# A two-layer encoder with product-key retrieval: eight more tokens take their down products from gathered rows, and half of a search moves ahead

## The reference, cut to what is computed

```python
def peer(h, w_q, sub_keys, w_down, w_up):
    q = (ht @ w_q).reshape(T, PEER_HEADS, 2, PEER_HALF_DIM)           # 8 heads, 2 halves of 128
    scores = jnp.einsum('thic,hikc->thik', q, sub_keys)               # 128 keys per half
    sv, si = lax.top_k(scores, PEER_TOPK)                             # 16
    cand = sv[:, :, 0, :, None] + sv[:, :, 1, None, :]
    best, ci = lax.top_k(cand.reshape(T, PEER_HEADS, 256), PEER_TOPK)
    ...
    expert = i1 * PEER_N_KEYS + i2                                    # 16384 experts, 128 of them per token
    gate = softmax(best)
    hid = gelu(einsum('cd,ckd->ck', x, w_down[expert]))
    return einsum('ck,ckd->cd', gate * hid, w_up[expert])
```

## Time and profile before

| | |
|---|---|
| time, median of 3 runs | 1514.79 us (1514.16 to 1517.17) |
| the profiled execution, its own time | 1503.53 us |
| its span, first to last instruction | 1501.7 us |
| TensorE busy | 1479.2 us, 98% |
| VectorE busy | 892.0 us, 59% |
| GpSimd busy | 716.5 us, 48% |
| DMA, whole span | 523.12 MB, mean 348 GB/s |
| mean granted TensorE clock | 0.997 |

### The profile page before, as it was taken

How to read it: one execution, slowest core, us unless ns; L and a number is a source line. 1 busy time by engine, 2 the same in 40 slices (tenths; PEclk the granted TensorE clock), 3 DMA queues, 4 the chain that set the end, 5 groups by cost and what they waited for, 6 DMA issues and landing times.

```text
span 1501.7 us, 29008 instructions
## 1 busy us (share of the span) xinstructions
PE 1479.2 (98%) x10648; PEld 1440.7 (96%) x10648; DVE 892.0 (59%) x2921; ACT 473.2 (32%) x1184; POOL 716.5 (48%) x632
## 2 busy tenths in 40 slices
PE   8999999999999999999999999999999999999996
PEld 6889999999999999999978999999999999999996
DVE  1740999948885444444623449997588834444363
ACT  6663231248881000000055533121788500000001
POOL 6577033448994333333467831333699723332350
PEclk9999999999999999999999999999999999999998
DMA  7356999999999999999845679999999999999993
GB/s 257 133 204 235 332 339 364 409 408 342 383 389 407 416 416 417 416 417 415 360 150 200 211 244 351 349 407 408 367 375 385 383 416 415 416 417 416 417 404 141
DMA packets 126416, 523.12 MB, mean 348 GB/s; under 512 B 14816, under 2 KB 15072, under 8 KB 109536
## 3 DMA queue, kind: packets, MB, share of 16 engines
q1 hardware_dynamic: 56896, 240.27, 42.0%
q0 software_dynamic: 55296, 201.35, 34.3%
q10 hardware_dynamic: 14112, 80.04, 13.1%
HBM read 519.48 MB, written 1.05 MB: 347 GB/s over the span
## 4 chain that ended last, share of the span: by engine, by line
PE 94%; POOL 1%; DMA 1%; issue 1%; ACT 1%; DVE 1%; DVEq 0%; POOLq 0%; SPq 0%; ACTq 0%
PE ps L992 93%; POOL w_lo L605 1%; DMA spare<-in_wu 1%; PE ps L1000 1%; ACT hT_hi L707 0%; DMA raw<-in_wm 0%; DMA xs<-in_x 0%; ACT w_hi L692 0%; ACT arena L680 0%; DVE arena L1385 0%; DVE rtmp L1374 0%; DVE arena L1523 0%; POOL arena L630 0%; PE ps L1322 0%; PE ps L1120 0%
## 5 line engine op out<-in xcount | busy, mean ns | idle before, releaser
L992 PE MATMUL ps<-arena,raw 128*128 128x160 f32 (+1 forms) x2688 | 377.4, 299 | 0.2
L992 PE MATMUL ps<-arena,w_raw 128*128 128x160 f32 (+1 forms) x2688 | 377.3, 299 | 0.0
L992 PEld LDWEIGHTS ps<-arena,raw 128*128 128x128 f32 x2688 | 368.1, 190 | 0.7 <-issue 0.7
L992 PEld LDWEIGHTS ps<-arena,w_raw 128*128 128x128 f32 x2688 | 368.2, 190 | 0.0
L622 POOL DMA_INDIRECT arena<-in_up_rows,ret x192 | 188.1, 979 | 355.1 <-DVE oh_buf L1697 263.3
L622 POOL DMA_INDIRECT arena<-in_rows,ret x192 | 200.0, 1042 | 285.8 <-ACT ret L879 104.5
L1697 DVE SCALAR_TENSOR_TENSOR oh_buf<-arena,ret,oh_buf 128x1024 f32<-128x1024 f32 x126 | 161.8, 1284 | 227.9 <-DMA arena<-in_up_rows,ret 227.9
L605 POOL TENSOR_TENSOR w_lo<-raw,w_hi 128x1024 fp32r<-128x1024 f32 x80 | 194.0, 2436 | 90.8 <-PE ps L992 66.1
L992 PE MATMUL ps<-arena 128*128 128x160 f32 (+5 forms) x1336 | 184.5, 302 | 0.4 <-DMA spare<-in_wu 0.3
L992 PEld LDWEIGHTS ps<-arena 128*128 128x128 f32 (+2 forms) x1336 | 177.9, 189 | 4.0 <-issue 2.6
L1580 DVE SCALAR_TENSOR_TENSOR arena<-arena,ps 128x1024 f32<-128x1024 f32 x128 | 153.6, 1213 | 0.0
(11 more groups left out here) (149 smaller groups left out, 1780.6 us busy)
## 6 DMA issues: line engine op xcount, KB each, us to landing
raw<-in_wd SPq DMA_DIRECT2D x92, 512.0 KB, 6.8
w_raw<-in_wd SPq DMA_DIRECT2D x92, 512.0 KB, 7.6
raw<-in_wm SPq DMA_DIRECT2D x80, 512.0 KB, 3.4
low_rows<-in_wu SPq DMA_DIRECT2D x18, 1024.0 KB, 7.9
arena<-in_wu SPq DMA_DIRECT2D x18, 1024.0 KB, 7.9
arena<-in_wd SPq DMA_DIRECT2D x32, 512.0 KB, 4.9
raw<-in_wu SPq DMA_DIRECT2D x14, 1024.0 KB, 8.0
raw<-in_wu ACTq DMA_DIRECT2D x14, 1024.0 KB, 8.0
```

Of the source, the lines that this page charges most:

```text
L992: return nc.tensor.matmul(out, lhsT, rhs, start=start, stop=stop, skip_group_check=shared)
```

## The change

There are four parts.

Tokens 96 to 103 (`MID` = 8) leave the down products and not the up products. Their hidden values come from 8 more gathered rows a layer, each of which serves the 8 tokens in 16 groups of partitions; the rows of the tokens are copied to these groups by 16 more transfers of SP, and their ids spread by one more matmul before the block at which the 32 tokens' ids are spread. The down products have 152 columns (`DOWN_COLS`). VectorE spreads the hidden values (`spread_mid`), TensorE brings them to one column per token beside down block 97 (`with_mid`), VectorE multiplies them onto the gates (`gate_mid`), and the last two of the 40 gate groups, which are now those of the eight tokens, are written in place of multiplied.

The search of the first tile is split into heads 0 to 3 and heads 4 to 7. The scores of the first four heads are made before query block 10, and VectorE searches them while the query blocks run. Banks are changed for it (`SCORE_BANKS`, `search_psum`). Gathers can begin after the first half: pieces of indices at ScalarE's blocks 4, 7, 20 and 25. 44 rows are dotted early, in 20 places, six of them in the second half of the first tile's search. TensorE's product of the 64 tokens' rows, before block 8, now waits for the first half.

The early spread of ids moves from block 28 to 26, the turning of gates and ids from 77 to 76, the gate groups from 80 to 79. The 60 later rows are dotted over 47 blocks, where 56 were over 44.

VectorE copies and splits ids of tokens from 96 on only, and ScalarE writes its ones from block 34 on, not 16.

```diff
-RING, IN_FLIGHT = 10, 5
+RING, IN_FLIGHT, RING_FIRST = 10, 5, 2
+MID, MID_TO = 8, DENSE_FROM + 8
+DOWN_ROWS = ROWS + MID
+GATHERS = DOWN_ROWS + ROWS
+DOWN_COLS = DENSE - MID
-IDS_AT = 77
-TAKE_AT = 26
-PIECES, PIECE_AT = 4, (18, 21, 24, 26)
-MORE_AT, MORE_TAKE_AT, MORE_GATES_AT = 28, 33, 40
+IDS_AT = 76
+TAKE_AT = 28
+PIECES, PIECE_AT = 4, (4, 7, 20, 25)
+EARLY_SCORES_BEFORE, EARLY_HEADS = 10, RH // 2
+SCORE_BANKS = (0, 1, 0, 1, 4, 5, 6, 7)
+MORE_AT, MORE_TAKE_AT, MORE_GATES_AT = 26, 34, 40
-G_FROM = 80
+G_FROM = 79
-ONES_FROM, ROWS_AT, ONES = 12, 8, 432
-SPARSE_FIRST, MORE_LAST = 18, 10
-EARLY, EARLY_PLACES = SPARSE_FIRST + MORE - MORE_LAST, 14
+ONES_FROM, ROWS_AT, ONES = 30, 8, 432
+SPARSE_FIRST, MORE_LAST = 26, 14
+EARLY, EARLY_PLACES = SPARSE_FIRST + MORE - MORE_LAST, 20
+DOT_BLOCKS = BLOCKS - G_FROM - 2
 def dots_after(b):
-    return EARLY + max(0, min(ROWS - EARLY, (b - G_FROM - 1) * (ROWS - EARLY) // 44))
+    return EARLY + max(0, min(DOWN_ROWS - EARLY, (b - G_FROM - 1) * (DOWN_ROWS - EARLY) // DOT_BLOCKS))
...
+                for i in range(MID_PARTS):
+                    sp.dma_start(mid_rows[i * MID:(i + 1) * MID, :],
+                                 gff[DENSE_FROM:MID_TO, :]).then_inc(mid_rows_sb, 16)
...
+                    if q == RING - 1:
+                        pool.wait_ge(first_searched, l + 1)
...
                 take_queries(0)
-                high_parts(l * LAYER + Q_FROM + 12, l * LAYER + MIX_BLOCKS)
+                act.wait_ge(rinv_done, query_norm)
+                for b in range(Q_FROM + 12, MIX_BLOCKS):
+                    high(b)
+                    if b == Q_FROM + EARLY_SCORES_BEFORE + 2:
+                        take_scores(0)
+                        take_scores(1)
                 take_queries(1)
...
+                    if b == EARLY_SCORES_BEFORE:
+                        pe.wait_ge(subk_loaded, 16 * (l + 1))
+                        pe.wait_ge(qT_sb, 8 * l + 4)
+                        score(0, range(2 * EARLY_HEADS))
...
+                for n in range(2 * EARLY_HEADS, HALVES, 4):
+                    pe.wait_ge(qT_sb, 8 * l + n // 2 + 2)
+                    pe.wait_ge(sc_sb, 8 * l + n // 4 - 1)
+                    score(0, range(n, n + 4))
+                pe.wait_ge(qT_sb, 8 * (l + 1))
+                score(1, range(HALVES))
...
+                    if with_mid:
+                        pe.wait_ge(mid_spread_done, l + 1)
+                        mm(mid_psum_of(slot), mid_rows[:, 0:P], mid_token).then_inc(mid_psum, 1)
                     out = down_psum(slot)
                     for c in range(DC):
-                        last = mm(out, block_in[:, c * P:(c + 1) * P], hT[:, c, :], c == 0, c == DC - 1)
+                        last = mm(out, block_in[:, c * P:(c + 1) * P], hT[:, c, MID:], c == 0, c == DC - 1)
...
                 pe.wait_ge(hng_done, l + 1)
-                pe.wait_ge(sc_sb, 8 * l + 4)
+                pe.wait_ge(pair_found, PIECES * l + PIECES // 2)
...
-                mm(ps[:, 5, 0:P], more_of, idf[:, 0, :]).then_inc(more_ids_psum, 1)
+                mm(ps[:, 5, 0:P], more_of, idf[:, 0, :])
+                pe.wait_ge(mid_of_done, l + 1)
+                mm(ps[:, 5, SEQ:SEQ + P], mid_of, idf[:, 0, :]).then_inc(more_ids_psum, 1)
...
+                search(0, 0, EARLY_HEADS, 2, 2, 3)
+                search(0, EARLY_HEADS, RH, 4, 5, 1)
+                gates_of(0)
+                search(1, 0, RH, 8, 5, 0)
+                gates_of(1)
```

More of the change, by code:

```diff
@@ L877, in take_picks @@
                         here, size = slice(half * SPARSE, (half + 1) * SPARSE), PICKS // PIECES
-                        first = half * PICKS + i * size
+                        first = (2 * i + half) * size
                         nc.scalar.activation(row_index[here, i * size:(i + 1) * size],
@@ L1171, in _, with score @@
                     transpose_half(xs, 4, hT_psum, k, HALF_BANKS)
+                def score(t, halves):
+                    for n in halves:
+                        o = n % 4 * P
+                        last = mm(ps[:, SCORE_BANKS[4 * t + n // 4], o:o + P], qT[:, n, t * P:(t + 1) * P],
+                                  subk[:, n, :])
+                        if n % 4 == 3:
+                            last.then_inc(sc_psum, 1)
                 for b in range(Q_BLOCKS):
@@ L1283, in _ @@
                 for g in range(TGROUPS):
-                    down(G_FROM + g)
+                    down(G_FROM + g, with_mid=g == MID_TURN)
                     token_gates(g)
@@ L1584, in _, with early_dot @@
                 early = [0]
-                def early_dot(t):
-                    if t:
-                        if not early[0]:
-                            dve.wait_ge(h_rows_psum, l + 1)
-                            dve.wait_ge(more_rows_sb, 16 * PARTS * (l + 1))
-                        dots(early_after(early[0] - 1), early_after(early[0]))
-                        early[0] += 1
-                for t in range(TILES):
-                    dve.wait_ge(sc_sb, 8 * l + 4 * (t + 1))
+                def early_dot():
+                    if not early[0]:
+                        dve.wait_ge(h_rows_psum, l + 1)
+                        dve.wait_ge(more_rows_sb, 16 * PARTS * (l + 1))
+                    dots(early_after(early[0] - 1), early_after(early[0]))
+                    early[0] += 1
@@ L1596, in _, with search @@
+                def search(t, h0, h1, ready, bank, dots_from):
+                    heads, halves = slice(h0, h1), range(2 * h0, 2 * h1)
+                    first_sv, first_id, pay = search_psum(bank, h1 - h0)
+                    dve.wait_ge(sc_sb, 8 * l + ready)
                     top16([(scores[t][:, n * KEYS:(n + 1) * KEYS], sv[:, t, n, :], si[:, t, n, :])
-                           for n in range(HALVES)], t)
+                           for n in halves], t, dots_from < 1)
                     settle()
-                    step(nc.vector.tensor_copy(sif[:, t].rearrange("p h i k -> p (h i) k"), si[:, t]))
@@ L1611, in _ @@
                         na = a1 - a0
-                        for dst, first, second in ((cand, first_sv, svt), (pay, first_id, sif[:, t])):
+                        for dst, first, second in ((cand[:, heads], first_sv, svt), (pay, first_id, ids)):
                             d = dst[:, :, o:o + na * nb].rearrange("p h (a b) -> p h a b", b=nb)
-                            f = first[:, :, a0:a1].unsqueeze(3).to_broadcast([P, RH, na, nb])
-                            s = second[:, :, 1, 0:nb].unsqueeze(2).to_broadcast([P, RH, na, nb])
+                            f = first[:, :, a0:a1].unsqueeze(3).to_broadcast([P, h1 - h0, na, nb])
+                            s = second[:, :, 1, 0:nb].unsqueeze(2).to_broadcast([P, h1 - h0, na, nb])
@@ L1626, in _ @@
+                    if h1 == RH:
+                        less.then_inc(best_done, 1)
+                    else:
+                        step(less)
                     eights = []
-                    for j in range(2 * RH):
+                    for j in range(2 * (h1 - h0)):
                         if j > 2:
                             dve.wait_ge(dve_step, eights[j - 3])
-                        h = j // 4 + j // 2 % 2 * (RH // 2)
+                        h = j // 2
                         for k in range(8):
-                            n = h * TOPK + j % 2 * 8 + k
+                            n = (h0 + h) * TOPK + j % 2 * 8 + k
```

225 lines of the change are left out of this document (151 added, 74 removed).

## The result

The changed kernel is slower: 1550.95 us (median of four executions, 1548.67 to 1553.61) against 1514.47 beside it, ratio 1.0238 with an interval of 1.0217 to 1.026. The profiled executions lie further apart, span 1550.1 against 1501.7: 48.4 us, where the medians differ by 36.5. The kernel before runs at 1503.9 us on some chips and at 1512.6 to 1516.7 on others; its one profile is of a 1503.5 us execution.

What follows compares the result with a forecast made beforehand. TensorE was taken as the bound (94% of the chain), the DMA next. Terms -26.2 + 6.0 + 0.4 + 1.5 + 0.6 = -17.7 us gave 1497.1 us against 1514.8; 8-in-10 range 1490 to 1506.

Steps and rivals of the forecast that it cites:

- The rows: Early gathers beside down weights: a row each 3.4 us, 44 rows ending near 309, no wait before block 76.
- The second search is the new bound: Rival: TensorE stands at block 76 until 44 rows are dotted, 14 us late twice, 1526 us; chance 0.05.
- Rows late: Rival: rows late at block 26 and the end of the up blocks, 5 us a layer more, 1507; chance 0.20.
- The width: Down products of 152 columns for 160: 6.4 ns off each record, 26.2 us in all, all on the path.
- width doesn't pay: Rival: 152 columns cost what 160 do, 2.5 us of small costs remain, 1517, no measurable change; chance 0.06.
- GpSimd in the gate stretch: Gate groups: GpSimd needs 3.175 us a group, TensorE 2.97, so TensorE waits more: +6.0 us in all.
- The search moved ahead: Vector's first-tile search starts near 132.8 instead of 151.9, done about 206.5; no wait, 0.4 us in all.
- The small ones: Extra id and hidden-value products: 0.6 us; the 16 copies' 11 us ahead of block 16's load hidden.
- The end of the up stretch: One to two MB handed from the down stretch to the up rows: +1.5 us in all, 0 to 10.

Runs made afterwards that it cites:

- e2: The changed kernel with odd down blocks 19 to 39 loaded from ScalarE's queue instead of SyncE's: ratio 1.0181 to the kernel before.
- e13: The changed kernel with the MID rows early and its 16 small copies replaced by a TensorE product and a ScalarE copy: ratio 1.0071.
- e16: The changed kernel with each of its 44 early gathers bringing half a row: not faster than the kernel before, span 1.0 us longer.
- e10: The changed kernel without dots between the steps of the first tile's second search, 44 early dots in 14 places instead of 20: ratio 1.0128.
- e3: The changed kernel with first indices taken behind block 18 instead of 4 and early dots in 14 places instead of 20: ratio 1.0273.
- e9: The changed kernel with odd blocks 19 to 39 on ScalarE's queue, early up loads behind block 39, no dots within the second search: ratio 1.0159.
- e12: The changed kernel with only the eight MID rows moved into the 44 early rows: ratio 1.0105.
- e14: The kernel of e13 with the last six of the 44 early dots behind the second tile's gates: 7 us slower in all.
- e1: The kernel before with only its down products cut from 160 to 152 columns: it gains nothing.
- e4: The changed kernel with the eight MID dots reading normed rows in PSUM instead of SBUF: 1.0198 by medians, interval too wide to tell.
- e6: The changed kernel with its 16 small copies issued one behind each of down blocks 20 to 35: no faster than the changed kernel.

## Why the prediction was wrong

**The step that failed is "The rows"**: "(408 - 253) GB/s leaves a row each 3.4 us", and from it "no wait". It gives the weights what they want and the rows the rest. Nothing in the kernel does that. While gathers were in flight the weights got 204 GB/s, and the rows 15.33 MB in 84 us, one each 2.9 us: they ended at 304.7, before the forecast's 309, and TensorE paid. The step also took 408 GB/s as given from 161 us on, where the copies left 248. It cost 44.3 us against the 0.4 to 1.9 forecast for it. e2 shows the share, e13 the copies, and e16 that none of it is left with half the bytes. The order of the bytes is the other half of it: rows that were taken 31 us before they were needed took the turns of weights that were needed at once, and e10, which takes them later, halves the early stalls. Where the order was mended, in e3, e9, e12 and e13, TensorE waited for the ids at block 76 instead, and e14 only moved that wait.

**"The second search is the new bound", the rival of 1526,** was priced at 0.05 and came nearest in time (1.007 by ratio), by luck: in kind it is what e3, e12 and e13 do, which stand at block 76 for the rows; in the changed kernel itself VectorE was 31 us early there. What stood against it, "the weights have a lead of eight blocks and the DMA held 408 GB/s", was the mistake: the lead was spent by block 24, and 408 is what the engines carry, not what a queue gets. "Rows late" named the right account, 10 MB against 7, and 5 us a layer in place of 22.

**The width** paid at the record: 7.0 ns each, 28.5 us against 26.2. Neither 0.13 ns a column (the Trainium skill's, cited there) nor "width doesn't pay" holds. "All of it is on the path, as the chain says" is what e1 refutes: the chain gives TensorE 94%, and the whole saving went into waits that had been a few us from showing.

**GpSimd in the gate stretch:** 4.6 us a layer alone (e1, e4), against 0.7 before: +7.8 in all, forecast 6.0. Mis-sized by a third. What was missed is the port: the MID dots read two SBUF operands, and cost GpSimd 6.2 us a layer, 12.4 in all. The diff says `mid_rows`, in `spare`; I counted the dots and not where they read. "The search moved ahead" and the early start held to 1 us. **The small ones:** the copies "hidden" behind a 33 us lead cost 7 to 8 us a layer (e13). That SyncE's 10.9 us of issue ahead of block 16 is the smaller part of it is suggested by e6, which moves them and gains nothing.

**The end of the up stretch:** +9.9 us where 1.5 was forecast; in layer 0 TensorE waited for the last up rows in every kernel with the eight more rows. It isn't the early rows' bytes: e16, with half of them, still waits 4.7 us there. In layer 1 the changed kernel's one long wait at the end, 1.3 us, was for up weights. What makes these rows and weights late stays open. e12's early stalls are some 5 us a layer below those of the changed kernel, with 44 early rows in both; its last early dot ends at 330.1 us and not at 304.7, so it may be e10's effect, which wasn't tested apart.

**The clock.** In the changed kernel, before its last 9 us, TensorE's clock was granted five times at its lower level, 1.2 of 2.4 GHz, for 3.4 to 10.2 us, beside waits of 1.0 to 4.0 us; in the kernel before, not once until its last 8 us. By the means of the two profiled executions, 0.988 and 0.997, this is some 14 us of the 48.4, counted in the stalls above. In layer 1, from 1000 to 1025 us, the mean is 0.80, (1.00 - 0.80) x 25 / 0.5 = 10 us of it (1.00 before):

```profile
1000.00:1025.00 25.00, 18.72 (x110) 17.66 (x109) 24.83 (x168) 5.36 (x14) 7.87 (x9) 0.80 1.01 392
```

It adds to the stalls: e13's wait of 6.95 us before block 76 costs 9.4.

## What to carry to other kernels

When a matrix engine and the transfers both run near full, an edit that speeds up the one is paid from the other: add up the bytes between two points, divide by the full rate, and compare with the engine's time there, before counting the saving. Then ask how the rate is shared, and when: a stream on one queue got half beside a second busy one here, not what it needed, and rows fetched long before their use took the place of weights that were due. And for each operation moved or added on VectorE, look where its operands lie: eight dots of two SBUF operands cost GpSimd 6.2 us a layer beyond their own time.

## What the hardware showed that I had not expected

- 16 copies of 32 KB from eight partitions to eight others kept the DMA engines' share at 1.02 while 248 GB/s were carried, gathers beside them included; without them 354.
- Beside dots of two SBUF operands two one-hots of GpSimd took 2.4 to 3.3 us in place of 1.59, and some gathers 1.73 to 1.76 in place of 1.03.
- Float32 records of 128, 152 and 160 columns start every 111.7, 129.0 and 135.9 ns: 0.72 and 0.86 ns a column, and no step between these three widths.
